# A recurrent mixer whose gates become tanh in the table of the exponential, with two pairs of first taps on another engine

## The reference, cut to what matters

```python
def block_diag_linear(x, w, b):            # 16 heads of 64
    return (jnp.einsum('bshi,hij->bshj', xh, w) + b).reshape(bsz, s, h * dh)

def rg_lru(x, w_a, b_a, w_x, b_x, lam):
    gate_a = jax.nn.sigmoid(block_diag_linear(xf, w_a, b_a))
    gate_x = jax.nn.sigmoid(block_diag_linear(xf, w_x, b_x))
    log_a = -LRU_C * gate_a * jax.nn.softplus(-lam)      # LRU_C = 8
    a = jnp.exp(log_a)
    mult = jnp.sqrt(-jnp.expm1(2.0 * log_a))
    bx = xf * gate_x * mult
    # h[t] = a[t] * h[t-1] + bx[t]

def recurrent_mixer(x, w_in, conv_w, conv_b, ...):
    y, r = jnp.split(x @ w_in, 2, axis=-1)
    y = jax.nn.gelu(y)
    r = causal_depthwise_conv(r, conv_w, conv_b)         # 4 taps
    h = rg_lru(r, ...)
    return (y * h) @ w_out
```

## Time and profile before

| | |
|---|---|
| median of three runs | 1483.22 us (1482.9 to 1483.72) |
| time of the profiled execution | 1483.2 us |
| its span, first to last instruction | 1481.4 us |
| granted TensorE clock | 1.0 of full speed in the whole span |
| busy share of the span | PE 98%, DVE 75%, ACT 55%, POOL 19% |
| the mixer's stretch | about 200 to 290 us |

### The profile page before, as it was taken

The page is one execution under the profiler, slowest core; times in us unless marked ns, Lnnn a source line. Parts: engine busy times, 40 slices in busy tenths (PEclk is TensorE's granted clock), DMA queues, the critical chain, the costliest instruction groups (busy, mean ns, idle before and its releaser), DMA issues.

```text
span 1481.4 us, 27773 instructions
## 1 busy us (share of the span) xinstructions
PE 1446.1 (98%) x9821; PEld 1333.1 (90%) x9821; DVE 1109.3 (75%) x2209; ACT 814.6 (55%) x1480; POOL 285.3 (19%) x348
## 2 busy tenths in 40 slices
PE   8999999999999999999999999999999999999998
PEld 7888899888888888899988888989999999899898
DVE  6776679877766777667777766997778769876883
ACT  6666458565645655444566545546644453675442
POOL 1111122311111111123311113412420124121000
PEclk9999999999999999999999999999999999999999
DMA  6657754565556665555566655533343554434343
GB/s 207 200 183 222 229 160 141 182 188 186 181 180 203 187 187 184 179 189 170 159 187 194 189 187 153 155 114 101 100 114 114 163 148 119 128 101 114 115 126 117
DMA packets 245557, 239.03 MB, mean 161 GB/s; under 512 B 15192, under 2 KB 244424, under 8 KB 245464
## 3 DMA queue, kind: packets, MB, share of 16 engines
q1 hardware_dynamic: 244888, 236.73, 52.3%
q10 hardware_dynamic: 576, 1.05, 0.2%
HBM read 236.70 MB, written 1.05 MB: 160 GB/s over the span
## 4 chain that ended last, share of the span: by engine, by line
PE 82%; DVE 12%; ACT 2%; issue 2%; DMA 1%; POOL 1%; SPq 0%; DVEq 0%; ACTq 0%; POOLq 0%
PE bank L612 73%; DVE w_lo L1683 3%; DVE work L2187 1%; PE bank L967 1%; ACT w_hi L1056 1%; PE bank L925 1%; DMA raw<-in_ffn_w_in_dram 1%; PE bank L907 1%; PE bank L890 1%; PE bank L973 1%; PE bank L836 1%; PE bank L983 1%; PE bank L846 1%; PE bank L906 0%; PE bank L926 0%
## 5 line engine op out<-in xcount | busy, mean ns | idle before, releaser
L612 PE MATMUL bank<-x_both,w_hi 128*128 128x512 f32 (+2 forms) x3552 | 805.3, 332 | 1.7 <-DVE h L1772 0.9
L1683 DVE TENSOR_TENSOR w_lo<-raw,w_hi 128x1024 fp32r<-128x1024 f32 (+1 forms) x456 | 552.0, 1234 | 220.6 <-ACT w_hi L1056 219.8
L1056 ACT CAST w_hi<-raw 128x1024 fp32r<-128x1024 f32 (+1 forms) x456 | 457.1, 1029 | 139.5 <-PE bank L612 122.1
L612 PEld LDWEIGHTS bank<-x_both,w_hi 128*128 128x128 f32 x3552 | 514.6, 189 | 5.2 <-DVE w_lo L1683 1.9
L612 PE MATMUL bank<-x_both,w_lo 128*128 128x256 f32 (+1 forms) x2480 | 496.9, 281 | 0.0
L612 PEld LDWEIGHTS bank<-x_both,w_lo 128*128 128x128 f32 x2480 | 432.4, 189 | 62.6
L612 PE MATMUL bank<-y_both,w_hi 128*128 128x512 f32 (+2 forms) x1472 | 345.7, 337 | 4.9 <-issue 3.5
L612 PEld LDWEIGHTS bank<-y_both,w_lo 128*128 128x128 f32 x1088 | 191.7, 188 | 31.3
L612 PEld LDWEIGHTS bank<-y_both,w_hi 128*128 128x128 f32 x1472 | 212.9, 189 | 5.6 <-issue 3.8
L612 PE MATMUL bank<-y_both,w_lo 128*128 128x256 f32 (+1 forms) x1088 | 215.8, 280 | 0.0
L1569 POOL TENSOR_TENSOR work<-work,rstd 128x256 f32<-128x256 f32 x88 | 63.5, 743 | 416.6 <-ACT work L1103 416.6
(11 more groups left out here) (306 smaller groups left out, 1246.9 us busy)
## 6 DMA issues: line engine op xcount, KB each, us to landing
raw<-in_ffn_w_in_dram SPq DMA_DIRECT2D x176, 512.0 KB, 3.8
raw<-in_w_in_dram SPq DMA_DIRECT2D x100, 512.0 KB, 3.6
raw<-in_ffn_w_out_dram SPq DMA_DIRECT2D x64, 512.0 KB, 4.7
raw<-in_w_out_dram SPq DMA_DIRECT2D x32, 512.0 KB, 4.3
raw<-in_ffn_w_out_dram SPq DMA_DIRECT2D x32, 384.0 KB, 3.5
raw<-in_rec_w_in_dram SPq DMA_DIRECT2D x16, 512.0 KB, 4.4
raw<-in_sg_w_in_dram SPq DMA_DIRECT2D x16, 512.0 KB, 4.3
raw<-in_rec_w_out_dram SPq DMA_DIRECT2D x8, 512.0 KB, 3.4
```

The costliest lines, as they stand in the source:

```text
L612: i_ = mm(accs[m][:, cols], w[:, s, j, m * P:(m + 1) * P], moving, start=begin and g == 0, stop=final)
L1056: nc.scalar.copy(w_hi[:, s, 0:n, :], raw[:, s, 0:n, :]).then_inc(hi_made, 1)
L1683: TT(w_lo[:, s, 0:n, :], raw[:, s, 0:n, :], w_hi[:, s, 0:n, :].bitcast(fp32), SUB).then_inc(lo_made, 1)
```

## The change

The sigmoid of each gate is written as (1 + tanh(z/2))/2. The biases are halved once (two more operations of 128x8 in the stage before). The decay's tanh and exp take the tanh of the gate with half the constant as scale and as bias, so that the addition of one is inside them. For the other gate one is added in one operation over four chunks (`one_more`, on ACT), and the factor 1/2 is put into the square root's scale (0.25). The first taps of the pairs 0 and 1 are made by ACT (`taps0`, during r = 1 and 3), and the further taps of these pairs stand on DVE during r = 2 and 4, after that unit's low half. On ACT the second four chunks' `decays` is taken apart: tanh before the cast of r = 11 and exp after it. On POOL the gated input stands behind the squares.

```diff
@@ -380,7 +380,8 @@
         conv_new, gates_mm, gates_sig, gated_in, ax_new, a2_new, mult2, mult_new = (
             sem(n) for n in ("conv_new", "gates_mm", "gates_sig", "gated_in", "ax_new", "a2_new", "mult2", "mult_new"))
 
-        rec_gelu, rec_bx, scanned = sem("rec_gelu"), sem("rec_bx"), sem("scanned")
+        rec_gelu, rec_bx, scanned, conv_tap0, gate_one = (
+            sem(n) for n in ("rec_gelu", "rec_bx", "scanned", "conv_tap0", "gate_one"))
 
         sg_gelu, sg_sqs, sg_sum, sg_rms = sem("sg_gelu"), sem("sg_sqs"), sem("sg_sum"), sem("sg_rms")
 
@@ -1188,33 +1189,50 @@
 
             pb = PHASES["rec_b"][1]
 
+            def taps0(p):
+
+                for c in (2 * p, 2 * p + 1):
+                    act.wait_ge(tile_read, 2 * pb + c + 1)
+                    activation(rec_x[:, c, :], rec_p[:, c, 0:SEQ], ACT.Identity, scale=pcol("rec_conv_w", c),
+                               bias=pcol("rec_conv_b", c)).then_inc(conv_tap0, 1)
+
             def gates(cs):
 
+                act.wait_ge(decay_v, 2)
                 for c in cs:
                     act.wait_ge(gates_mm, c + 1)
-                    for k, (dst, b) in enumerate(((rec_a, "rec_gate_a_b"), (rec_g, "rec_gate_x_b"))):
-                        activation(dst[:, c, :], bank[4 + c % 4][:, k * SEQ:(k + 1) * SEQ], ACT.Sigmoid,
-                                   bias=pcol(b, c)).then_inc(gates_sig, 1)
-
-            def decays(cs):
-
-                act.wait_ge(decay_v, 2)
+                    for k, (dst, b) in enumerate(((rec_a, 5), (rec_g, 6))):
+                        activation(dst[:, c, :], bank[4 + c % 4][:, k * SEQ:(k + 1) * SEQ], ACT.Tanh, scale=0.5,
+                                   bias=decay[:, b, c:c + 1]).then_inc(gates_sig, 1)
+
+            def decay_tanhs(cs):
+
                 act.wait_ge(gates_sig, 2 * cs[-1] + 2)
                 if cs[0]:
                     act.wait_ge(mult2, 4)
                 for c in cs:
-                    activation(rec_t[:, c % 4, :], rec_a[:, c, :], ACT.Tanh, scale=decay[:, 3, c:c + 1]).then_inc(ach, 1)
+                    activation(rec_t[:, c % 4, :], rec_a[:, c, :], ACT.Tanh, scale=decay[:, 3, c:c + 1],
+                               bias=decay[:, 3, c:c + 1]).then_inc(ach, 1)
                 chain[0] += len(cs)
+
+            def decay_exps(cs):
+
                 act.wait_ge(ach, chain[0])
                 for c in cs:
-                    activation(rec_a[:, c, :], rec_a[:, c, :], ACT.Exp, scale=decay[:, 2, c:c + 1]).then_inc(ax_new, 1)
+                    activation(rec_a[:, c, :], rec_a[:, c, :], ACT.Exp, scale=decay[:, 2, c:c + 1],
+                               bias=decay[:, 2, c:c + 1]).then_inc(ax_new, 1)
+
+            def one_more(cs):
+
+                r = rec_g[:, cs[0]:cs[-1] + 1, :]
+                activation(r, r, ACT.Identity, bias=ones[:, 0:1]).then_inc(gate_one, 1)
 
             def mult():
 
                 for b in (0, 4):
                     act.wait_ge(mult2, b + 4)
                     r = rec_p[:, b:b + 4, 0:SEQ]
-                    activation(r, r, ACT.Sqrt).then_inc(mult_new, 1)
+                    activation(r, r, ACT.Sqrt, scale=0.25).then_inc(mult_new, 1)
 
             def gelu(c, n):
                 act.wait_ge(tile_read, 2 * (pb + 4) + c + n)
@@ -1228,21 +1246,29 @@
             r = 0
             for p in range(8):
                 for U, _, _ in units_of(pb + p):
+                    if r == 11:
+                        decay_tanhs(range(4, 8))
                     if r == 13:
                         gelu(0, 4)
                     split_w(U + LEAD)
+                    if r == 11:
+                        decay_exps(range(4, 8))
+                    if r == 12:
+                        one_more(range(4, 8))
                     if r == 13:
                         upper(range(4))
                     if r == 1:
                         root(1, META)
+                    if r in (1, 3):
+                        taps0(r // 2)
                     if r == 5:
                         gates(range(4))
                     if r == 7:
-                        decays(range(4))
+                        decay_tanhs(range(4))
+                        decay_exps(range(4))
+                        one_more(range(4))
                     if r == 8:
                         gates(range(4, 8))
-                    if r == 10:
-                        decays(range(4, 8))
                     if r == 12:
                         mult()
                     if r == 14:
@@ -1578,14 +1604,14 @@
             h_squares(1, "out01", META)
 
             for b in (0, 4):
-                for c in range(b, b + 4):
-                    pool.wait_ge(gates_sig, 2 * c + 2)
-                    TT(rec_x[:, c, :], rec_x[:, c, :], rec_g[:, c, :], MUL).then_inc(gated_in, 1)
                 if b:
                     pool.wait_ge(mult2, 4)
                 for c in range(b, b + 4):
                     pool.wait_ge(ax_new, c + 1)
                     TT(rec_s[:, c % 4, :], rec_a[:, c, :], rec_a[:, c, :], MUL).then_inc(a2_new, 1)
+                pool.wait_ge(gate_one, b // 4 + 1)
+                for c in range(b, b + 4):
+                    TT(rec_x[:, c, :], rec_x[:, c, :], rec_g[:, c, :], MUL).then_inc(gated_in, 1)
             h_squares(2, "rec_out", META)
             gate_scale(1)
             h_squares(3, "out02", META)
@@ -1854,8 +1880,11 @@
                 if unit == 13:
                     link(TS(decay[:, 8, :], lam, -1.0, 0.0, MUL, MAX))
                     link(TT(decay[:, 9, :], decay[:, 8, :], decay[:, 4, :], ADD))
-                    TS(decay[:, 2, :], decay[:, 9, :], -8.0, None, MUL)
-                    TS(decay[:, 3, :], decay[:, 9, :], 8.0, None, MUL).then_inc(decay_v, 1)
+                    TS(decay[:, 2, :], decay[:, 9, :], -4.0, None, MUL)
+                    for k, n in ((5, "rec_gate_a_b"), (6, "rec_gate_x_b")):
+                        t, r, _ = PAR[n]
+                        TS(decay[:, k, :], par[:, t, r:r + NC8], 0.5, None, MUL)
+                    TS(decay[:, 3, :], decay[:, 9, :], 4.0, None, MUL).then_inc(decay_v, 1)
 
             out_phase("out01", lambda c: pcol("mix_norm", c), SPLITS["x_rec_b"], second=decays_of_lambda)
 
@@ -1867,13 +1896,17 @@
                 for k in range(4):
                     for c in (2 * p, 2 * p + 1):
                         src, w = rec_p[:, c, k:k + SEQ], pcol("rec_conv_w", k * NC8 + c)
+                        if k == 0 and p < 2:
+                            continue
                         if k == 0:
                             i_ = TS(rec_x[:, c, :], src, w, pcol("rec_conv_b", c), MUL, ADD)
                         else:
+                            if k == 1 and p < 2:
+                                dve.wait_ge(conv_tap0, c + 1)
                             i_ = STT(out=rec_x[:, c, :], in0=src, scalar=w, in1=rec_x[:, c, :], op0=MUL, op1=ADD)
                         if k == 3:
                             i_.then_inc(conv_new, 1)
-                    if k < 3:
+                    if k < 3 and (k or p >= 2):
                         link(i_)
 
             def mult_squares(cs):
@@ -1916,6 +1949,9 @@
                         split_w(U + LEAD)
                     if r == 1:
                         inverse(1, META)
+                    if r in (2, 4):
+                        dve.wait_ge(tile_read, 2 * pb + r)
+                        conv1(r // 2 - 1)
                     if r == 12:
                         scans(range(4))
                     if r == 13:
@@ -1929,7 +1965,7 @@
                         for m in range(2):
                             c = 2 * (p % 4) + m
                             scaled(pb + p, m, rec_p[:, c, 3:3 + SEQ] if p < 4 else rec_y[:, c, :], SEQ, META)
-                        if p < 4:
+                        if p in (2, 3):
                             dve.wait_ge(tile_read, 2 * (pb + p) + 2)
                             conv1(p)
                     r += 1
```

## The result

The median after is 1486.44 us (18 runs, 1485.65 to 1486.85) against 1482.57 for the kernel before, measured beside it (18 runs, 1481.41 to 1483.91): a ratio of 1.0025, 95% interval 1.0018 to 1.0032, or 3.7 us (2.7 to 4.7). The forecast was 1486.1, its own range 1485.3 to 1487.0. The whole interval lies above 1, so the kernel became slower. The ratio lies just beyond the 0.2% that the prediction drew as its line, and the low end of the interval just inside it. The medians themselves differ by 3.9 us, where 2.9 was forecast.

A forecast was written before the change was run, and what follows sets the result against it. PE bounds the kernel, waiting on the mixer's ACT and DVE tail: unit 16's low half at 255.7 against 252.87, +2.85, with the collision +2.9, gives 1483.2 + 2.9 = 1486.1 us; likeliest 1485.3 to 1487.0, with rivals 1 and 2 1482.9 to 1487.7.

The forecast's parts named there:

- the 0.2% that the prediction drew as its line: Whole kernel: about 0.2% (3.0 us, up to 1486.2) is what can be told from no change.
- What bounds: Mixer to output projection: lateness at PE's first stop, before unit 16, is late at the end, one for one.
- the likeliest case: Whole kernel: the forecast mechanism holds, 1485.3 to 1487.0 us; the forecast has chance 0.70.
- Part 1: Mixer's first taps on ACT, convolutions behind the weight split: gate products late by 1.9, 3.0, 2.85, 2.85 us.
- Part 2: Gates by tanh on ACT: three table loads go, 3.85 us of ACT, only the last on the path.
- Part 3: ACT's tail: second operands and addition (1.16) less a load (1.28) and overlaps cost 0.45; first root 3.3 us late.
- Rival 3: Gate tanh takes another table than exp, so one load of 1.28 us stays on the path: 1487.4; chance 0.05.
- Part 4: POOL's products behind the squares: second four from 249 to about 252, one collision of 0.55 us with DVE counted.
- Rival 1: Gates not late, first products before 213.2; about -0.2 us, 1483.0, not slower; chance 0.10.
- Rival 2: POOL's second products, started after 250.5, fall on DVE's four: 2.2 us, low half of unit 16 +4.4, 1487.6; chance 0.12.
- What would show it: Trace signs: first products about 214.8, PE idle 1.9 and 1.3 us, first projection unit near 258.7, its idle as before.

The follow-up runs named there:

- e2: The kernel before with only the first taps of two pairs on ACT and their two convolutions moved; 1485.74 us, ratio 1.0018 against before.
- e3: The changed kernel with the two convolutions ahead of that unit's low half on DVE, taps still on ACT; 1482.93 us, ratio 1.0001 against before.
- e1: The changed kernel with the first taps back on DVE and the convolutions where they stood; 1482.99 us, ratio 1.0003 against before.
- e5: e3 with the second addition of one right after the gates and POOL's second products ahead of its squares; 1481.80 us, ratio 0.9993 against before.
- e4: e3 with (1 + tanh) times x as one DVE operation per chunk, without ACT's additions and POOL's eight products; 1481.36 us, ratio 0.999 against before.
- e6: The taps back on DVE as in e1, the gating on DVE as in e4; 1481.41 us, ratio 0.9993 against before.
- e7: e4 with the casts of r = 11 and 13 ahead of tanh and gelu on ACT; 1481.52 us, ratio 0.999 against before.

## Why the prediction was right, and where it was off

**What bounds.** That a delay at unit 16 is a delay at the end held: +3.33 there and +3.4 at the end. The time, 1486.44 where 1486.1 was forecast, agrees better than the step: before's median was 0.65 lower beside after than the 1483.22 that the sum began with, so the difference of 3.9 is 1.0 more than the forecast 2.9, just over the 3.8 at the top of the likeliest case's range. That the time came out within 0.4 is in part luck. The chances, 0.50 for the same and 0.47 for slower, were no clear call either.

**Part 1, right.** The forecast delays of the four products were 1.9, 3.0, 2.85 and 2.85; the marks give 1.92, 3.06, 2.90 and 2.78. The first wait did not add to the second. The mechanism is shown twice: e2 makes the delay with this part alone, and e3 takes it away by swapping two lines on DVE.

**Part 2, right.** Before has seven table loads between 203 and 275 us, after has four; three went, and the load ahead of the roots (248.06) follows the exponentials and the addition directly. Rival 3 is out.

**Part 3, right.** The root was forecast 3.3 late and is 3.16 late, 0.38 of it beyond the gates where 0.45 was written (0.48 in e1, where the gates are not late). The step had tanh and exp at 0.50 each: four take 2.08. The addition, put at 1.16, took 1.15. The cast of unit 16 was to end at 255.65; it ends at 253.65 + 1.03 + 0.77 = 255.45 on before's times.

**Part 4, the term that was mis-sized.** "POOL's four end at about 252, so I count one." POOL started its second products at 248.9 on before's times, as forecast (249), but four of them took 4.42 us, so they ended at 253.3, and they met three of DVE's products, not one. Line 1614 in the trace of after (duration ns min/median/max) has the price that I had left out, POOL's own share of the collisions:

```profile
L1614 POOL TENSOR_TENSOR work<-work x8: 915/919/1723, 232.7 to 251.6; 128x256 f32<-128x256 f32 x8
```

I had taken POOL's four at about the shortest, 0.734 each, and charged the collision to DVE alone, though the same row of before shows a maximum of 1.72. In the trace of after the second four take 0.97, 1.72, 0.92 and 0.92 us; the 1.72 lies beside the low half, the last two beside DVE's products. In e5 the same four are 0.74, 0.74, 1.72 and 0.74: alone, or begun ahead of DVE's operation, a product takes what I had assumed. On the path: DVE's four products cost 2.71 - 1.42 = 1.29 more, and DVE is free for the low half at 255.44, which is 256.21 on before's times. The cast's end at 255.45 would have held it without collisions, so 0.53 of the 1.29 is covered and 0.76 counts: 255.45 - 252.87 = 2.58, and 0.76 to it makes 3.34, the 3.33 of the marks. e5 measures the same term by taking the overlap away, at 0.59 with a root 0.14 later. For this reason the forecast of 2.9 was 0.4 low at unit 16; the interval of the medians' difference (2.7 to 4.7) holds both.

The Trainium skill, page "SBUF — State Buffer", section "SBUF: two separate sides", has the shared port as a lock for a whole instruction. The trace agrees that both sides wait, POOL's four products taking 4.42 here and DVE's 2.71 together; but a DVE product waited 0.55 at most (0.96 less 0.41), less than the 0.73 of a POOL product, because POOL's was already under way: in the trace of after one of POOL's ran from 250.75 to 251.67 and the DVE product beside it from 250.99 to 251.95. So by a whole product per collision the loss would be overstated, and the measured 0.55 decides. (The prediction wrote that a collision of 0.734 would be covered just barely; its own slack, 0.65 to 0.7, was less than that.)

**The rivals.** Rival 1 needed the first products before 213.2; they came at 214.8 on before's times. Its world is e3, where the products are not late, and there the time is before's within the noise: 0.3 above the kernel beside it, where the rival had 0.2 below. Rival 2 was half there: its condition, POOL's start after 250.5, was not met, but POOL's length did what its start did not.

**What would show it.** The waits of PE were 1.76 and 1.11 (forecast 1.9 and 1.3). Unit 16 started at 259.18 on before's times, where 258.7 was written, and its idle time was 2.74 where "about as before (2.2)" was: the 0.5 of the collisions, in both.

## What to carry to other kernels

Work that moves to an engine with time to spare takes its place in that engine's queue: what stood behind that place, here a weight cast with a low half and a convolution in a chain behind it, inherits the wait. Before moving an operation, list what is queued behind its new place and who waits for that; swapping the order of two lines on the waiting engine (e3) gave back all that the move had cost (3.37 us at the low half of unit 16). And where two engines disturb each other, lengthen the operations of both before counting how many overlap.

## What the runs showed of the hardware that was not expected

The granted TensorE clock fell to half, from 2.4 to 1.2 GHz, at unit 16 of after, which began behind 2.74 us of idle PE. Windows of 1 us of after (columns: PE, PEld, DVE, ACT, POOL busy with counts, then PEclk, DMA share, GB/s):

```profile
258.00:259.00 1.00, 0.59 (x3) 0.62 (x4) 1.00 (x4) 1.00 (x3) 0.00 (x0) 0.75 0.89 298
259.00:260.00 1.00, 1.00 (x7) 1.00 (x7) 1.00 (x4) 0.36 (x1) 0.00 (x0) 0.50 0.50 174
260.00:261.00 1.00, 1.00 (x6) 1.00 (x6) 1.00 (x1) 0.93 (x2) 0.00 (x0) 0.50 0.08 16
261.00:262.00 1.00, 1.00 (x7) 1.00 (x6) 1.00 (x4) 1.00 (x2) 0.00 (x0) 0.55 0.00 0
262.00:263.00 1.00, 1.00 (x11) 1.00 (x10) 1.00 (x3) 0.59 (x1) 0.00 (x0) 1.00 0.70 153
```

Six or seven matmuls a window instead of eleven: unit 16 took 4.44 us instead of 2.94. It cost nothing here, since the 0.51 and 0.86 us for which PE had waited in before ahead of units 19 and 20 (the latter in the earlier trace rows) are gone in its place: PE begins unit 20 at +3.3, and the low halves of the units stay at +3.3. Over the profiled runs, at unit 16: with 2.74 us of idle time the clock fell each time (after and e1 for 3.4 us; e3 for 6.8, from 0.8 before the idle time was over); behind 2.2 us it fell in e2 and did not in before and e5; behind 1.0 us (e4, e6, e7) it did not fall. In e3 PE begins unit 20 without a wait at +0.84, though its low half stands at -0.05, and the next norm's sum is at +0.57. So there the fall seems to cost half a microsecond, though no run had the longer fall alone to show it.

The length of the idle time does not decide it alone. All nine profiled executions have a wait of PE of 1.80 us near 970 us; within 1.6 us after it the clock fell, for 3.4 us, in five of them (after, e1, e2, e5, e6), and not in the other four. Why stays open.

Also unexpected was POOL's side of a collision: a product of 128x256 takes 0.74 alone (e5), 0.92 beside one of DVE's products of that shape and 1.72 beside a low half of 128x1024, while the low half goes from 1.2 to 1.63 or 1.79 (e5) and 1.76 (after). What is under way is not lengthened: POOL's last product in e5, from 240.25 to 240.99, took 0.74 although a low half began beside it at 240.28, and that low half took the 1.79.
